# Feed-forward up projections as seven block products instead of eight, with weight sums on GpSimd and the other sums on VectorE

## The reference

```python
def causal_dwconv(x, w, b):            # along the tokens, K = 3
    K, T = w.shape[0], x.shape[1]
    xp = jnp.pad(x, ((0, 0), (K - 1, 0), (0, 0)))
    y = b + xp[:, 0:T, :] * w[0]
    for j in range(1, K):
        y = y + xp[:, j:j + T, :] * w[j]
    return y

def conv_glu_ffn(xn, w_up, conv_w, conv_b, w_down):
    u, gt = split_cols(xn @ w_up, (D_FF, D_FF))       # D_FF = 2752
    u = causal_dwconv(u, conv_w, conv_b)
    return (jax.nn.silu(u) * gt) @ w_down
```

## Time and profile before

| | |
|---|---|
| time, median of 3 runs | 2202.91 us (2202.4 to 2203.11) |
| profiled execution, first to last instruction | 2200.9 us |
| TensorE busy | 2067.1 us (94%) |
| VectorE busy | 617.4 us (28%) |
| ScalarE busy | 365.2 us (17%) |
| GpSimd busy | 111.3 us (5%) |
| chain that ended last | TensorE 73%, DMA 24%, VectorE 1%, ScalarE 1% |
| ten full groups of a feed-forward, group 10 behind them | 139.1 us, 10.4 us |

### The profile page before, as it was taken

One profiled execution on the slowest core, in us unless ns is written; L12 is line 12 of the kernel. 1 busy time (PEld: TensorE's weight loads), 2 busy tenths in 40 slices (PEclk: granted clock), 3 DMA queues, 4 the chain that ended last, 5 costly groups with the idle time before them and its releaser, 6 DMA issues.

```text
span 2200.9 us, 27233 instructions
## 1 busy us (share of the span) xinstructions
PE 2067.1 (94%) x11446; PEld 1366.0 (62%) x11446; DVE 617.4 (28%) x1252; ACT 365.2 (17%) x691; POOL 111.3 (5%) x186
## 2 busy tenths in 40 slices
PE   9999999999999999999999999977699999999765
PEld 7888788888888888888778633322243334433222
DVE  5445432335464134353343321100011111111001
ACT  4322132000042121000232400100000000010000
POOL 0123000000000000000000000100000000001000
PEclk9999999999999999999999999988899999999888
DMA  7221443435524345357335489999999999999996
GB/s 271 103 78 41 160 166 115 153 144 230 206 77 176 145 177 191 144 196 315 153 123 192 155 345 427 428 427 427 427 427 419 427 426 427 426 392 427 426 427 265
DMA packets 44434, 587.61 MB, mean 267 GB/s; under 512 B 5344, under 2 KB 5616, under 8 KB 9360
## 3 DMA queue, kind: packets, MB, share of 16 engines
q1 hardware_dynamic: 44304, 585.79, 65.6%
HBM read 584.72 MB, written 1.05 MB: 266 GB/s over the span
## 4 chain that ended last, share of the span: by engine, by line
PE 73%; DMA 24%; DVE 1%; ACT 1%; issue 0%; SPq 0%; PEld 0%; DVEq 0%; PEldq 0%; ACTq 0%
PE pb L410 72%; DMA ring<-in_gu 11%; DMA ring<-in_dne 6%; DMA arena<-in_dne 4%; DMA arena<-in_gu 3%; PE pb L420 1%; DVE arena L327 0%; DMA ring<-in_ab_small 0%; ACT arena L371 0%; DVE arena L321 0%; DVE ring L312 0%; DVE arena L312 0%; SPq L590 0%; ACT arena L377 0%; DVE cst L312 0%
## 5 line engine op out<-in xcount | busy, mean ns | idle before, releaser
L410 PE MATMUL pb<-arena,ring 128*128 128x256 f32 (+2 forms) x2784 | 604.1, 380 | 2.1 <-ACT arena L371 2.0
L410 PEld LDWEIGHTS pb<-arena,ring 128*128 128x128 f32 (+2 forms) x2784 | 516.7, 189 | 81.2 <-issue 7.5
L410 PE MATMUL pb<-arena 64*64 64x64 f32 (+12 forms) x2996 | 402.9, 347 | 18.7 <-DMA ring<-in_dne 10.8
L410 PEld LDWEIGHTS pb<-arena 64*64 64x64 f32 (+5 forms) x2996 | 276.3, 156 | 128.9 <-issue 94.5
L410 PE MATMUL pb<-arena,cst 128*64 128x512 f32 (+6 forms) x1108 | 281.0, 623 | 59.0 <-DMA ring<-in_gu 56.8
L410 PE MATMUL pb<-ring,cst 128*64 128x512 f32 (+2 forms) x800 | 255.8, 627 | 0.0
L410 PEld LDWEIGHTS pb<-arena,cst 128*64 128x64 f32 (+4 forms) x1108 | 91.0, 142 | 231.6 <-issue 229.3
L410 PE MATMUL pb<-ring,arena 128*64 128x512 f32 (+3 forms) x544 | 159.3, 570 | 4.4 <-DMA arena<-in_dne 4.4
L377 ACT ACTIVATE arena<-pb 128x512 f32<-128x512 f32 (+2 forms) x128 | 66.0, 516 | 517.9 <-PE pb L420 423.1
L319 DVE TENSOR_SCALAR arena<-pb 128x512 f32<-128x512 f32 x30 | 20.8, 692 | 465.6 <-PE pb L410 465.6
L371 ACT ACTIVATE arena<-arena 128x512 f32<-128x512 f32 (+6 forms) x151 | 87.7, 581 | 297.0 <-DVE arena L327 271.0
(11 more groups left out here) (149 smaller groups left out, 1474.3 us busy)
## 6 DMA issues: line engine op xcount, KB each, us to landing
arena<-in_gu SPq DMA_DIRECT2D x64, 2048.0 KB, 19.2
ring<-in_gu SPq DMA_DIRECT2D x50, 2048.0 KB, 19.4
arena<-in_dne SPq DMA_DIRECT2D x30, 2048.0 KB, 19.4
ring<-in_dne SPq DMA_DIRECT2D x21, 2048.0 KB, 19.4
kv<-in_gu SPq DMA_DIRECT2D x14, 2048.0 KB, 18.5
ring<-in_up SPq DMA_DIRECT2D x13, 2048.0 KB, 7.8
kv<-in_dne SPq DMA_DIRECT2D x9, 2048.0 KB, 19.4
ring<-in_ada SPq DMA_DIRECT2D x8, 2048.0 KB, 8.0
```

What stands on the lines that cost most here:

```text
L410: r = self.e.matmul(out, lhsT, rhs, start=start, stop=stop, skip_group_check=True)
```

## The change

For groups 0 to 9 of both layers, the product of the 1024 x 512 weights of a group with the 1024 x 256 activations is cut into two-by-two blocks. The channel blocks are split into even and odd (index `e`), the columns into `u` and gate (index `h`), the tokens into two halves of 128 (index `i`). Eight block products become seven (the Winograd form), and sums stand around them:

- GpSimd makes four sums of 128x1024 of a group's weights (`weight_sums_g`). Three go to spare places in `kv` and `arena`, one over a block of the unit itself. It works up to two groups ahead: for group g it waits for `used` of group g-2 (`ffn_g`).
- VectorE makes four sums of activations of 128x512 once for each layer (`row_sums_v`), ahead of the sum of the squares.
- TensorE makes 56 matmuls of 128x128 for a group in place of 32 of 128x256 (`seven_p`), into four banks `a` to `d` for each group. All eight banks are used in turn until group 10, which goes back to bank 0.
- ScalarE copies the first product out of PSUM (`first_product_s`), one 256-wide copy for each group.
- VectorE adds the products: four operations of 256 with one operand in PSUM ahead of the convolution (`first_half_v`), three ahead of the gate's product (`second_half_v`). The root is now multiplied in behind them, by a 512-wide operation whose operands are both in SBUF, twice for each group.

Group 10 is made as before.

```diff
+        def row_sums_v(V, n):
+            V.wait_ge(f"{n}.x3")
+            s1, s2, s3, s4 = (XSUM[:, k] for k in range(4))
+            V.tt(s1, XA[1][0], XA[1][1], ADD)
+            V.tt(s2, s1, XA[0][0], SUB)
+            V.tt(s3, XA[0][0], XA[1][0], SUB)
+            V.tt(s4, XA[0][1], s2, SUB)
+            V.mark(f"{n}.sums")
+
+        def weight_sums_g(G, unit, spare):
+            b = corners(G.unit(unit)[:, 0:4096])
+            t1, t2, t4 = spare
+            G.tt(t1, b[0][1], b[0][0], SUB)
+            G.tt(t2, b[1][1], t1, SUB)
+            G.tt(b[0][1], b[1][1], b[0][1], SUB)
+            G.tt(t4, t2, b[1][0], SUB)
+            G.mark(f"{unit}.sums")
+
+        def seven_p(P, unit, n, spare, xn, after_first=None):
...
+            bank = P.tile(n + "a")
+            product(bank, 0, b[0][0], XA[0][0], ready=xn)
+            product(bank, 1, b[1][0], XA[0][1], sig=n + "a")
+            if after_first is not None:
+                after_first()
+            bank = P.tile(n + "b")
+            P.wait_ge(f"{xn}.sums", f"{unit}.sums")
+            product(bank, 0, t2, s2)
+            product(bank, 1, b[0][1], s3, sig=n + "b")
+            bank = P.tile(n + "c")
+            product(bank, 0, t4, XA[1][1], sig=n + "c")
+            bank = P.tile(n + "d")
+            product(bank, 0, t1, s1)
+            product(bank, 1, b[1][1], s4, sig=n + "d")
+            P.used(unit)
...
+        def first_half_v(V, n, k, out):
+            a = halves_of(V.tile(n + "a"))
+            V.wait_ge(n + ".first")
+            V.tt(out[:, :, 0:128], FIRST[:, k], a[:, 1], ADD)
+            b = halves_of(V.tile(n + "b"))
+            V.tt(HALF_SUM[:, 0], FIRST[:, k], b[:, 0], ADD)
+            V.free(n + "a")
+            V.tt(HALF_SUM[:, 1], HALF_SUM[:, 0], b[:, 1], ADD)
+            V.free(n + "b")
+            c = halves_of(V.tile(n + "c"))
+            V.tt(out[:, :, 128:256], HALF_SUM[:, 1], c[:, 0], SUB)
+            V.free(n + "c")
+
+        def second_half_v(V, n, out):
+            d = halves_of(V.tile(n + "d"))
+            V.tt(out[:, :, 0:128], HALF_SUM[:, 0], d[:, 0], ADD)
+            V.tt(out[:, :, 0:128], out[:, :, 0:128], d[:, 1], ADD)
+            V.tt(out[:, :, 128:256], HALF_SUM[:, 1], d[:, 0], ADD)
+            V.free(n + "d")
...
+        def ffn_g(G, n):
+            G.begin(f"ffn{n}")
+            G.wait_ge(f"xa{n}.o3")
+            for g in range(SEVENS):
+                if g > 1:
+                    G.wait_ge(f"used up{n}.{g - 2}")
+                weight_sums_g(G, f"up{n}.{g}", SPARE[n][g % 2])
...
+            P.main, P.i = list(range(8)), 0
+            for g in range(SEVENS):
+                seven_p(P, f"up{n}.{g}", f"{f}.p{g}", SPARE[n][g % 2], f, None if g else lambda: added_p(P, f))
+            P.main, P.i = [0, 1, 2, 3], 0
...
+                if g < SEVENS:
+                    first_half_v(V, f"{f}.p{g}", g % 2, UB)
+                    V.tt(UB, UB, bc(RB, 1, 2), MUL)
+                else:
+                    b = V.tile(f"{f}.u{g}")
+                    normed(b, tiles)
...
+                if g < SEVENS:
+                    second_half_v(V, f"{f}.p{g}", UB)
+                    V.tt(UB, UB, bc(RB, 1, 2), MUL)
+                else:
+                    normed(V.tile(f"{f}.g{g}"), [t for t in tiles if t[1] == 128])
+                    V.free(f"{f}.g{g}")
```

More of the change, by code:

```diff
@@ L831, in proj_tok_p, with corners @@
             P.used(unit)
+        XT4 = XT_.rearrange("p (q e t) -> p q e t", q=4, e=2)
+        XA = [[XT4[:, :, e, i * 128:(i + 1) * 128] for e in range(2)] for i in range(2)]
+        XSUM = MX_.rearrange("p (s q t) -> p s q t", s=4, q=4)
+        HALF_SUM, FIRST = (XS_[:, o:o + 512].rearrange("p (s j t) -> p s j t", s=2, j=2) for o in (1024, 1536))
+        def corners(w):
+            q = w.rearrange("p (q e n) -> p q e n", q=4, e=2)
+            return [[q[:, :, e, h * 256:(h + 1) * 256] for h in range(2)] for e in range(2)]
@@ new lines, in seven_p, with product @@
+        def seven_p(P, unit, n, spare, xn, after_first=None):
+            b = corners(P.unit(unit)[:, 0:4096])
+            t1, t2, t4 = spare
+            s1, s2, s3, s4 = (XSUM[:, k] for k in range(4))
+            def product(bank, half, lhs, rhs, sig=None, ready=None):
+                for j in range(2):
+                    o = half * 256 + j * 128
+                    for q in range(4):
+                        if ready is not None:
+                            P.wait_ge(f"{ready}.x{q}")
+                        P.mm(bank[:, o:o + 128], lhs[:, q, j * 128:(j + 1) * 128], rhs[:, q, :], q == 0, q == 3,
+                             sig=sig if (j, q) == (1, 3) else None)
+            bank = P.tile(n + "a")
[13 more added lines that the diff above has]
+            P.used(unit)
@@ new lines, in halves_of, with first_product_s @@
+        def halves_of(b):
+            return b.rearrange("p (h j t) -> p h j t", h=2, j=2)
+        def first_product_s(S, n, k):
+            a = halves_of(S.tile(n + "a"))
+            S.copy(FIRST[:, k], a[:, 0])
+            S.mark(n + ".first")
+        def first_half_v(V, n, k, out):
[10 more added lines that the diff above has]
+            V.free(n + "c")
@@ L2332, in ffn_s @@
             for g, (w2, tiles) in enumerate(FFN):
-                S.reach(f"{f}.g{g}")
+                if g < SEVENS:
+                    if g > 1:
+                        S.wait_ge(f"free {f}.p{g - 2}a")
+                    first_product_s(S, f"{f}.p{g}", g % 2)
+                else:
+                    S.reach(f"{f}.g{g}")
                 cb = CB2[g % 2]
@@ L2353, in normed @@
             def normed(b, tiles):
[L2355 to L2359, removed]
+                for q, (c1, cw) in enumerate(tiles):
+                    V.tt(UB[0:cw, q, :], b[0:cw, q * 256:(q + 1) * 256], RB[0:cw], MUL)
             for g, (w2, tiles) in enumerate(FFN):
@@ L2374, in ffn_v @@
                 V.mark(f"{f}.c{g}")
-                normed(V.tile(f"{f}.g{g}"), [t for t in tiles if t[1] == 128])
-                V.free(f"{f}.g{g}")
+                if g < SEVENS:
+                    second_half_v(V, f"{f}.p{g}", UB)
+                    V.tt(UB, UB, bc(RB, 1, 2), MUL)
+                else:
+                    normed(V.tile(f"{f}.g{g}"), [t for t in tiles if t[1] == 128])
+                    V.free(f"{f}.g{g}")
                 for q, (c1, cw) in enumerate(tiles):
```

16 lines of the change are left out of this document (9 added, 7 removed).

## The result

The changed kernel takes 2251.28 us (median of 4 runs, 2250.96 to 2254.3), the kernel before in the same sitting 2203.01 us (4 runs, 2202.4 to 2204.22). The ratio is 1.0219, 95% interval 1.0205 to 1.0233: slower by 48 us. Predicted were 2231 us and a range of 2190 to 2262; the forecast's own part of that range ended at 2243.

The account below looks back on a forecast made before the run. The prediction took VectorE, held up by GpSimd's sums, to become the bound in place of TensorE. Layers cost +13.5 and +15.3 us: 2200.9 + 28.8 = 2229.7, plus 2.0 for the median, about 2231 us; range 2190 to 2262.

Parts of the forecast that it names:

- the forecast's own part of that range: Whole kernel: 2216 to 2243 us, from cover between 0.9 and 2.6 and the clock; given 60%.
- TensorE's gain: Up projections: 56 matmuls at 0.223 us make 12.5 us a group, 1.3 us less than before.
- the rival's 2187: Up projections: TensorE stays the bound if exclusion costs VectorE under about 3.7 us a group; 2187 us, chance 12%.
- GpSimd's work: Weight sums: 2.35 us each undisturbed, 9.6 us a group with gaps, under 12.5, so GpSimd's speed doesn't pace the groups.
- The exclusion: VectorE and GpSimd instructions both reading two SBUF streams exclude each other whole: 2.05 us lost each, 8.2 a group.
- Off that goes what VectorE does meanwhile with one SBUF operand: at least the two `ts`: Cover against the 8.2 us: 0.9 for two `ts`, at most the seven PSUM sums as well, 3.3.
- the walk: Layer 0 step by step over both engines: VectorE paces at 16.0 us, group 10 starts at 509.0 against 498.2.
- the rival "dearer": Up projections: cover of 0.9 throughout, +6.8 a layer, 2245 us; or slower GpSimd weight reads, 2263 us; chance 20%.
- VectorE's own work: Up projections: VectorE alone needs 8.8 us a group; 85.9 us for ten groups less the part behind the last bank.
- The start: Layer 0: TensorE waits 2.2 us for the squares, root at 369.8, VectorE then waits 1.7 us for b and c.
- Layer 1: Second layer's feed-forward: VectorE's first sum waits 1.8 us more than in layer 0, so +15.3 us.
- Bank 0 ahead of group 10: Group 10 needs the bank of group 9's product d: TensorE stands 10 us, then 1.7 us of clock.

Follow-up runs that it names:

- the runs with ten such groups in which VectorE all but keeps up: Changed kernel with half-width weight sums, 2194.78 us; memsets for sums, 2193.7; sums on VectorE, group 10 from bank 1, squares before row sums, `ts` on ScalarE, 2190.1.
- five groups and the squares first: Changed kernel with five seven-product groups a layer, all banks in turn until group 10, squares' inputs added before the row sums: 2195.97 us, ratio 0.9966.
- the run with two groups: Changed kernel with seven products for groups 0 and 1 alone, groups 2 to 10 as in the kernel before: 2216.54 us, ratio 1.0058.

## Why it came out so

- *TensorE's gain: right.* Records 0.112 us apart, 12.5 us a group; the runs with ten such groups in which VectorE all but keeps up are at 2190 to 2195, near the rival's 2187.
- *GpSimd's work: right.* 2.35 us for a free sum, up to 2.88 when VectorE was in first; it never paces TensorE.
- *The exclusion: right in kind and in price, and it decides the sign.* The locked period is 17.07 us; less the 8.98 that VectorE needs alone, that is 8.1 us for four GpSimd sums, 2.02 each (predicted 2.05). Memsets in the sums' place cost nothing, half-width sums nothing that reaches the end. The sums with an operand in PSUM run beside GpSimd, as said.
- *The step that failed: "Off that goes what VectorE does meanwhile with one SBUF operand: at least the two `ts`".* `ts` waits like the rest (2.33 us in place of 0.41). Of the 8.2 us the walk took off 1.75 a group, 0.9 of it for the `ts`, which gave nothing; the sums with an operand in PSUM gave the other part, 0.8. So VectorE lost 7.3 us a group and not 6.45: 58.7 against 51.6 us, 7 us a layer. That is the price of the rival "dearer" with a cover of 0.9 throughout (2245 us), which had 20%. The forecast on its own, 2216 to 2243, misses the 2251; the stated range holds it by that rival.
- *VectorE's own work: 2 us a layer too small.* A group takes 8.98 us and not 8.8, so its ten groups less the last products are 87.9 us and not 85.9. From the root (371.0 less the 1.1) the sum is 369.9 + 3.15 + 87.9 + 58.7 = 519.65, and group 10 starts at 519.6; the walk had 509.0.
- *The start: mis-sized by a little.* The root came as predicted (369.9), the wait for the squares too (1.99 for 2.2 us). But b took 3.53 us and not 1.95 at the lower clock, so that VectorE waited 3.15 us for b and c; the walk had 1.7, and the prediction about 1 more for the clock. TensorE's wait of 1.2 us in group 0 for ScalarE's activations costs nothing: product a ends at 364.3, less the 1.1, as walked.
- *Layer 1:* +15.3 predicted, +26.1 measured (23.8 at group 10, 2.3 behind it), with the same 17 us period; its squares waited 4.4 us (4.0 by the prediction's terms). Both layers together are 49.9 us where 28.8 were predicted. With the 1.1 of drift and less the 2.3 that the expert stage takes back, for which the prediction had no term, that is the 48.7.
- *Two slips that don't bear on it.* The walk steps TensorE at 12.4 us where the text has 12.5, and 2229.7 + 2.0 is 2231.7.
- *Bank 0 ahead of group 10: right.* 9.05 us of wait (10 predicted) and 2.4 us of clock behind it (1.7 predicted). That it was avoidable by one number stood in the walk and was not drawn out of it.

The kernel before had rows that could have warned of `ts`, and I looked at none of them. Lines by form over its whole span (busy us, mean ns):

```profile
L312 DVE TENSOR_TENSOR arena<-arena 128x256 f32<-128x256 f32 x46 | 19.6, 425 | 15.9 <-ACT arena L371 11.5
L312 DVE TENSOR_TENSOR arena<-pb,arena 128x256 f32<-128x256 f32 x44 | 18.7, 425 | 31.7 <-PE pb L410 29.1
...
L321 DVE TENSOR_SCALAR arena<-arena,col 128x256 f32<-128x256 f32 x42 | 17.3, 413 | 1.5
...
L321 DVE TENSOR_SCALAR arena<-pb,col 128x256 f32<-128x256 f32 x8 | 4.3, 544 | 5.2 <-ACT arena L377 4.7
...
L321 DVE TENSOR_SCALAR arena<-arena 128x512 f32<-128x512 f32 x2 | 0.9, 427 | 0.1
...
L319 DVE TENSOR_SCALAR arena<-arena 128x1024 f32<-128x1024 f32 x1 | 0.7, 695 | 0.0
```

A `tt` of 256 takes 425 ns whether it reads PSUM or not. The `ts` of this stage, with column scalars, takes 544 ns from PSUM and 413 from SBUF, 131 less for 256 elements. Without column scalars it goes from 427 to 695 ns between 512 and 1024 elements, half a nanosecond for each, where `tt` goes from 692 to 1224 ns, twice that. So these rows fit two elements at a time between SBUF and SBUF, and a `ts` that uses two streams although it has one operand; by themselves they don't show the streams. The Trainium skill states the rest ("SBUF — State Buffer", section "Who interferes with whom"): `tensor_scalar` is among the operations that can enter a two-port mode and then contend with GpSimd; and ("VectorE: DVE Perf Modes", section "Mode 2×_2P — use both read ports for one tensor") that this holds at fp32, between SBUF operands. The trace agrees: 2.33 us for 0.41. I had counted operands where this rule counts ports. The Trainium skill also states ("SBUF — State Buffer", the same section) that an operation with two SBUF inputs contends with a GpSimd instruction that reads SBUF and not with one that only writes; the run with memsets agrees, with the 1.75 us above for three such operations.

## What to carry to other kernels

Before work is handed to GpSimd to relieve VectorE, price each GpSimd instruction with two SBUF operands on VectorE's account too, at nearly its full length (2.0 us of 2.35 here), unless VectorE has PSUM operands to work on in that time; where VectorE does it in half the time, as here, keep it there. An engine that is 4 us slower a group than the one it serves shows nothing until the buffers' lead is used up, and all of it from then on: with five groups of this kind TensorE waited for no bank, with ten it did from group 5 on. Put what the other engine waits for first, and don't restart a ring of banks on the one that is given back last; undone one at a time, the two were 8 and 20 us of the 48 here.

## What the runs showed of the hardware

- A GpSimd tensor_tensor in SBUF holds up VectorE's `ts` (one SBUF operand and column scalars, 128x256, fp32): 2.33 us for 0.41, in all six cases of layer 0 in which it began while a sum ran. A GpSimd memset of 128x1024 (0.95 us) held up none of the `stt` and `tt` that ran beside it; what it does to a `ts` stays open.
- The loss is one-sided. VectorE lost 2.02 us to a GpSimd sum (17.07 less 8.98, for four); GpSimd's sums among VectorE's back-to-back work took 2.35 to 2.42 us mostly, 2.88 at most.
- TensorE's waits of only 2.0 to 4.4 us were mostly followed by a lower granted clock (0.83 to 0.91 in windows of 14 to 20 us), so that 16 records take 2.95 us for 1.95; with five groups and the squares first, without the waits of 2.0 and 4.1 us, the same windows are at 1.00. Not always: behind a wait of 2.3 us in layer 1 the window from 830 to 850 us has 0.91 in the run with half-width sums and 1.00 in the run with memsets, and behind a wait of 2.0 us in layer 0 the window from 366 to 380 us has 1.00 in the run with two groups. What tells these apart I didn't find.
